# Decode attention of a hybrid decoder layer: one step list for three engines against a list for each, with the token transposes in another PSUM bank

## The reference

```
ckv_past = ckv_pool[page_table]; kpe_past = kpe_pool[page_table]
s = (q_abs . ckv_past + q_pe . kpe_past) * ATTN_SCALE
p = softmax(concat(s, s_new)); o_lat = p[past] . ckv_past + p[new] . ckv
```

```
sa = S . kk ;  S = S * d - sa x b + v x k ;  o = S . r
```

## Time and profile before

| | us |
|---|---|
| median of 3 runs (lowest, highest) | 2041.21 (2038.88, 2041.49) |
| profiled execution, its own time | 2037.07 |
| its span, first to last instruction | 2035.4 |
| TensorE busy | 1865.2 (92%) |
| VectorE busy | 895.6 (44%) |
| ScalarE busy | 494.7 (24%) |
| mean granted TensorE clock | 0.970 |

### The profile page before, as it was taken

The page is one execution under the profiler, slowest core; times in us unless marked ns, Lnnn a source line. Parts: engine busy times, 40 slices in busy tenths (PEclk is TensorE's granted clock), DMA queues, the critical chain, the costliest instruction groups (busy, mean ns, idle before and its releaser), DMA issues. The chain is left out here.

```text
span 2035.4 us, 45818 instructions
## 1 busy us (share of the span) xinstructions
PE 1865.2 (92%) x19360; PEld 1164.3 (57%) x19360; DVE 895.6 (44%) x1984; ACT 494.7 (24%) x1164; POOL 172.6 (8%) x158
## 2 busy tenths in 40 slices
PE   4899999999987999899949999999999879998898
PEld 2565676666654666654326656766666546665543
DVE  2024134222766676654230340332318577775542
ACT  3111012222412333311131110222224123333201
POOL 0010000011334000000000100000212240000000
PEclk9899999999999999979989999999999899999899
DMA  9500000000205666341075001010001166562411
GB/s 388 207 11 27 21 21 32 21 21 13 59 26 159 185 188 180 109 178 42 32 301 213 0 27 32 11 32 22 21 22 50 28 186 186 176 186 83 178 42 42
DMA packets 103927, 191.18 MB, mean 94 GB/s; under 512 B 17162, under 2 KB 87260, under 8 KB 100004
## 3 DMA queue, kind: packets, MB, share of 16 engines
q1 hardware_dynamic: 103716, 188.19, 27.9%
HBM read 175.41 MB, written 21.19 MB: 97 GB/s over the span
## 5 line engine op out<-in xcount | busy, mean ns | idle before, releaser
L771 PE MATMUL PB<-RB,R 128*128 128x344 f32 x1632 | 496.1, 457 | 0.0
L771 PEld LDWEIGHTS PB<-RB,R 128*128 128x128 f32 x1632 | 303.7, 191 | 159.6 <-issue 19.7
L1946 PE MATMUL PB<-RB,R 128*128 128x512 f32 x512 | 221.2, 593 | 0.0
L1589 PE MATMUL PB<-WUQ,Q 32*32 32x256 f32 x5120 | 191.0, 385 | 14.7 <-DVE WUQ L1748 9.4
L1748 DVE STREAM_TRANSPOSE WUQ<-RB 128x512 f32<-128x512 f32 x316 | 197.0, 676 | 5.5 <-DMA RB<-in_cache 5.3
L1946 PEld LDWEIGHTS PB<-RB,R 128*128 128x128 f32 x512 | 97.0, 190 | 120.8 <-issue 118.6
L931 ACT ACTIVATE R<-PB 128x344 f32<-128x344 f32 x90 | 41.2, 457 | 423.4 <-PE PB L771 423.4
L1184 DVE TENSOR_TENSOR PB<-PB,CST 128x128 f32<-128x128 f32 x64 | 18.8, 294 | 226.3 <-PE PB L791 226.3
L1589 PEld LDWEIGHTS PB<-WUQ,Q 32*32 32x32 f32 x5120 | 90.0, 104 | 46.0 <-DVE WUQ L1748 23.1
L619 PE MATMUL PB<-RB,R 128*128 128x344 f32 x288 | 88.5, 472 | 10.8 <-PEq L225 10.8
L619 PEld LDWEIGHTS PB<-RB,R 128*128 128x128 f32 x288 | 57.1, 199 | 41.4 <-issue 14.8
(11 more groups left out here) (355 smaller groups left out, 2619.6 us busy)
## 6 DMA issues: line engine op xcount, KB each, us to landing
RB<-in_cache SPq DMA_DIRECT2D x512, 160.0 KB, 2.6
R<-in_w_ada SPq DMA_DIRECT2D x16, 1536.0 KB, 17.4
R<-in_w_in SPq DMA_DIRECT2D x44, 512.0 KB, 3.7
RB<-in_w_out SPq DMA_DIRECT2D x8, 1024.0 KB, 9.9
RB<-out_x_stream SPq DMA_DIRECT2D x2, 4096.0 KB
out_x_stream<-RB SPq DMA_DIRECT2D x16, 512.0 KB
RB<-in_x_prompt SPq DMA_DIRECT2D x1, 4096.0 KB
RB<-in_w_kv SPq DMA_DIRECT2D x2, 1280.0 KB, 5.6
```

The source lines that it names most:

```text
L771: mm = pe.matmul(jobbank(j)[:, 0:CH], ring[:, blkno[n] % 4, k, :], hT[:, k, chunk(c)], start=(k == 0), stop=(k == KT - 1))
L1589: mm = pe.matmul(PB[qp[o], 2 * (h % 2) + q % 2, 0:256], Q4[qp[q], g, :], k[qp[q], c], start=(g == 0), stop=(g == NB - 1), skip_group_check ...
L1946: mm = pe.matmul(PB[0:n, 2 * (t % 2) + hf, :], mixT[:, k, cols(t)], wo[:, k, hf * 512:(hf + 1) * 512], start=(k == 0), stop=(k == 5))
```

## The change

The one list becomes three (`PE_PAIR`, `DVE_PAIR`, `ACT_PAIR`), each walked by its own engine, with the words of one pair of heads repeated 8 times; `PT-` and `PV-` are those of the odd head of the pair before, `PT0` and `PV0` those of the pair's even head, and `T20`, `T21` are the first two turns of the next pair. TA writes bank 4 and not bank 6. The scaling of the state into `Sg` becomes a step G of its own, without drains but in the last pair, and the second part of the level masks becomes a step LV. The page slots (`QS`, `HB`) and SyncE's list are as before.

```
-            STEPS = [...]
-            chain = ("Z", "U", "H", "O")
-            plan = []
...
+            chain = ("Z", "U", "H", "G", "O")
+            PE_PAIR = (
+                "S00 S01 S02 MA Z0 S03 S04 U0 PT- S05 S06 H0 X1 S07 Z1 Y1 S08 U1 S09 S10 H1 X2 PV- Y2 S11 S12 S13 OO "
+                "X3 S14 PT0 S15 Y3 S16 S17 X4 AK TA Y4 S18 TB S19 X5 PV0 Y5"
+            ).split()
+            DVE_PAIR = (
+                "T02 T03 T04 T05 T06 MA T07 LV H0 T08 T09 T10 Y1 G0 T11 T12 MX0 H1 T13 Y2 T14 T15 T16 T17 T18 Y3 T19 "
+                "T20 G1 AK Y4 T21 MX1"
+            ).split()
+            ACT_PAIR = (
+                "Z0 U0 MA PT- X1 Z1 U1 X2 EX0 OO X3 PT0 X4 TA TB X5 EX1 Y5"
+            ).split()
+            def pair_plan(words):
+                out = []
+                for p in range(NS):
+                    for w in words:
+                        if w[0] in "ST" and w[1] in "012":
+                            out.append((2 * p + int(w[1]), w[0], int(w[2])))
+                        elif w[:2] in ("PT", "PV", "MX", "EX"):
+                            out.append((2 * p - 1 if w[2] == "-" else 2 * p + int(w[2]), w[:2], 0))
+                        else:
+                            out.append((p, "rw", w))
+                return [x for x in out if 0 <= x[0] < NH] + TAIL
...
                         elif n == "TA":
-                            pe.wait_ge(ak_done, p + 1)
+                            pe.wait_ge(pp_done, 2 * p + 1)
                             for f in range(2):
-                                pe.transpose(PB[:, 6, f * P:(f + 1) * P], A2[...], ident)
+                                pe.transpose(PB[:, 4, f * P:(f + 1) * P], A2[...], ident)
...
                         elif n == "TB":
-                            pe.wait_ge(ta_done, p + 1)
+                            pe.wait_ge(ak_done, p + 1)
...
                         if n[0] == "Z":
+                            pe.wait_ge(ta_done, p + 1)
                             pe.wait_ge(tb_done, p + 1)
...
-                    for h, what, g in plan:
+                    for h, what, g in pair_plan(PE_PAIR):
...
                         (PT, TensorE)
                             if h:
                                 pe.wait_ge(pp_done, h)
+                            if h % 2:
+                                pe.wait_ge(ta_done, h // 2 + 1)
...
                         (VectorE)
                             dve.transpose(Tm..., Tc...).then_inc(tm_done, 1)
+                        elif n == "LV":
                             levels(2, LEVELS).then_inc(bm_done, 1)
...
+                        elif n[0] == "G":
+                            i = 2 * p + int(n[1])
                             if i + 1 < NCH:
-                                dve.drain()
+                                if p == NS - 1:
+                                    dve.drain()
                                 dve.tensor_tensor(Sg, S0[:, (i + 1) % 4], ecol..., ALU.mult)
+                                if p == NS - 1:
+                                    dve.drain()
...
-                        elif what == "S":
-                            if NB * h + g + 2 < NB * NH:
-                                turn(NB * h + g + 2)
+                        elif what == "T":
+                            turn(NB * h + g)
```

More of the change, by code:

```diff
@@ L1402, in bass_hybrid_trunk @@
             fcol = lambda rb: RP + 32 * rb if rb < 8 else 32 * (rb - 8)
-            STEPS = ["MA", "Z0", "X1", "U0", "Y1", "H0", "X2", "Z1", "Y2", "U1", "X3", "H1", "Y3", "OO",
-                     "X4", "AK", "Y4", "TA", "X5", "TB", "Y5"]
-            chain = ("Z", "U", "H", "O")
-            plan = []
[L1410 to L1421, removed]
@@ L1422, in bass_hybrid_trunk @@
-            plan += [(NH - 1, "PT", 0), (NS, "rw", "Z0"), (NH - 1, "PV", 0), (0, "FC", 1), (NS, "rw", "U0"), (0, "FC", 2), (NS, "rw", "H0"),
-                     (0, "FC", 3), (NS, "rw", "Z1"), (0, "FC", 4), (NS, "rw", "U1"), (0, "FC", 5), (NS, "rw", "H1"), (0, "FC", 6),
-                     (NS, "rw", "OO")]
+            chain = ("Z", "U", "H", "G", "O")
[3 more added lines that the diff above has]
+            ).split()
@@ L1426, in bass_hybrid_trunk @@
+            TAIL = [(NH - 1, "PT", 0), (NS, "rw", "Z0"), (NH - 1, "PV", 0), (0, "FC", 1), (NS, "rw", "U0"), (0, "FC", 2), (NS, "rw", "H0"),
+                    (NS, "rw", "G0"), (0, "FC", 3), (NS, "rw", "Z1"), (0, "FC", 4), (NS, "rw", "U1"), (0, "FC", 5), (NS, "rw", "H1"),
+                    (0, "FC", 6), (NS, "rw", "OO")]
             with nc.Block() as block:
@@ L1477, in prepare @@
                         elif n == "TA":
-                            pe.wait_ge(ak_done, p + 1)
+                            pe.wait_ge(pp_done, 2 * p + 1)
                             for f in range(2):
-                                pe.transpose(PB[:, 6, f * P:(f + 1) * P], A2[:, f, p * P:(p + 1) * P], ident)
+                                pe.transpose(PB[:, 4, f * P:(f + 1) * P], A2[:, f, p * P:(p + 1) * P], ident)
                             for f in range(2):
-                                mm = pe.transpose(PB[:, 6, (2 + f) * P:(3 + f) * P], pT[:, 2 + f, p * P + 1:(p + 1) * P + 1], ident)
+                                mm = pe.transpose(PB[:, 4, (2 + f) * P:(3 + f) * P], pT[:, 2 + f, p * P + 1:(p + 1) * P + 1], ident)
                             mm.then_inc(ta_full, 1)
                         elif n == "TB":
-                            pe.wait_ge(ta_done, p + 1)
+                            pe.wait_ge(ak_done, p + 1)
                             for f in range(2):
@@ L1645, in prepare @@
                             act.wait_ge(ta_full, p + 1)
-                            t6 = PB[:, 6, :].rearrange("p (v f w k) -> p v f w k", v=2, f=2, w=2)
+                            t4 = PB[:, 4, :].rearrange("p (v f w k) -> p v f w k", v=2, f=2, w=2)
                             for c in range(2):
                                 for w in range(2):
-                                    op = act.activation(TOK[k][hp[w], 0:2, 2 * c:2 * c + 2, :], t6[hp[c], :, :, w, :], ACT.Identity)
+                                    op = act.activation(TOK[k][hp[w], 0:2, 2 * c:2 * c + 2, :], t4[hp[c], :, :, w, :], ACT.Identity)
                             op.then_inc(ta_done, 1)
@@ L1677, in follow @@
                             act.activation(A3[:, :, p * P:(p + 1) * P], PB[:, 6, 0:2 * P].rearrange("p (f t) -> p f t", f=2), ACT.Identity).then_inc(oo_done, 1)
-                    for h, what, g in plan:
+                    for h, what, g in pair_plan(ACT_PAIR):
                         if what == "rw" and g[0] in chain:
@@ L1792, in follow @@
                             op.then_inc(st_done, 1)
+                        elif n[0] == "G":
+                            i = 2 * p + int(n[1])
                             if i + 1 < NCH:
-                                dve.drain()
+                                if p == NS - 1:
+                                    dve.drain()
                                 dve.tensor_tensor(Sg, S0[:, (i + 1) % 4], ecol[:, :, i + 1:i + 2].broadcast_to([P, 2, 64]), ALU.mult)
-                    for h, what, g in plan:
+                                if p == NS - 1:
+                                    dve.drain()
+                    for h, what, g in pair_plan(DVE_PAIR):
                         if what == "rw" and g[0] in chain:
```

## The result

| | before | after |
|---|---|---|
| median (lowest, highest), us | 2040.92 (2038.88, 2041.49) | 2165.31 (2159.60, 2167.62) |
| profiled execution, its span | 2037.07, 2035.4 | 2159.60, 2157.9 |
| mean granted TensorE clock | 0.970 | 0.936 |

The changed kernel takes 1.0611 times as long (95% interval 1.0593 to 1.0628). It was forecast at 2167, slower.

A forecast was written before the change was run, and what follows sets the result against it. Taken as bound by when pages come, through a ring of two loads in series: 2037.1 + 94.8 (ring) + 31 (lower clock) = 2163 us, with 4.1 for the median 2167; range 2108 to 2200.

The forecast's parts named there:

- Bound by when pages come: Decode stage: page loads start when PV frees their slot and take 15.9 us; slack before the turn is only 3.7 us.
- The ring: Decode stage: PV0, load, T10, PV-, load, T20, back to PV0; loads in series, 37.2 us a pair against 28.96.
- Its size: Length of a decode pair: two loads of 15.9 us, 5.4 from turns to PVs, 2.4 for the lower clock.
- The fixed point: First layer, counted from pair 0's T20 at 650.46: PV0 at 653.4, pair 7's T10 at 892.5; 47.4 us a layer.
- The clock: Decode steps after TensorE's stops run partly at the lower clock: 2.4 us a pair, 31 us in both layers.
- The 44 us that I worked out by its formula: Decode stages: clock loss of 26 stops by the skill's formula, 44 us in place of 31, so 2181.
- The smaller edits: Decode stage: three lists save up to 2.9 us a pair, single score blocks cost 0.4; all hidden while pages are late.
- "faster" rival: Decode stage: pages come in time, TensorE's waits decide, 46 us of waits go: 1995; chance 0.05.
- Short loads: Decode page loads: each takes the shortest seen, 14.3 us, and the clock stays up; 42 us less, 2094; chance 0.09.

## Why the prediction was right, step by step

- **Bound by when pages come.** Right. The slack before T10 and T20 (3.7 us in the pair read, 1.7 to 5.3 in all) was all there was; all 26 gated loads now end 0.12 to 0.13 us before the turn that waits for them, which is the hand-over alone.
- **The ring.** Right, and shown from four sides: open it at PV-, at PV0 or at T20 and 75 to 95 of the 125 us go; open it at both PVs and all go; shorten the loads and 26 times the shortening goes, and some of the clock's part with it. T10 was not moved by itself.
- **Its size.** 2 x 15.9 + 5.4 + 2.4 = 39.6 us a pair was forecast, 39.74 measured, but two parts missed and cancelled. The steps at the lower clock cost more: from PV to first issue 2.72 us in each load (1.94 before), and 6.95 us for the two ways from turn to PV (3.41 and 3.54), where 5.4 was priced at the upper clock. That is 3.1 us for the clock where 2.4 was taken. The loads took less: from first issue to last page 13.54 us (13.95 before), 0.8 us in a pair. That the total came within 2 us of 2167 is in part luck.
- **The fixed point.** T20 of pair 0 came at 648.89 (forecast 650.46), the first turn of the stage being 2.0 us sooner; PV0 followed at 652.3 (653.4), and T10 of pair 7 at 906.05 (892.5, and some 15.6 for the clock: 908).
- **The clock.** Right in kind. On the steps of the ring it cost 3.1 us a pair, some 40 us over 13 pairs, where 31 was taken; filling the stops gave 21 us net of longer loads. After every stop, not after 0.6 of them, 0.50 was granted: behind the 26 stops at gated turns for 3.4 us in 5 cases and for 6.8 in 21. The Trainium skill (TensorE: Matmul & The Clock Gate, "HAM oscillation — how this bites in real kernels") says that a DMA wait which comes back in each tile lets the clock fall again each time. The trace agrees, 26 times in 26. The 44 us that I worked out by its formula (2136 + 44 is 2180, not the 2181 written) took 3.4 us for every stretch; with the measured lengths, 160 us in all, the formula gives an estimate of 80 us, far above the 40 seen in the ring. Part of a low stretch passes while TensorE stands still (it is busy for 5.68 of the 6.80 us from 785.30), and part over steps behind PV's first half, which are not in the ring.
- **The smaller edits.** Wrong, where it did not count: I wrote that the three lists save up to 2.9 us of waits in a pair and that single blocks cost 0.4. With pages in time the waits are 0.9 us less and the stops marked "issue" 1.7 us more, and nothing that can be measured is saved (0.999). My "faster" rival at 1995 therefore never had its price, whatever the loads did.
- **Short loads.** The rival's 14.3 us didn't come; of the 1.6 us that it wanted a load was 0.4 us shorter from first issue to last page, and the lower clock before the first issue took that back twice over.

## What to carry to other kernels

When a step that frees a buffer is moved in a hand-written order, follow the buffer all the way round: free, load, first use, everything queued behind the first use, and back to the step that frees. If the sum of a round is longer than the period, the engines' busy shares say nothing; and where two buffers' rounds pass through each other's waiting instructions, their loads add. Put nothing that a later "free" depends on behind a first use in any queue: one turn moved past three steps gave 95 of 125 us. A free step also has an earliest place, behind the copy that it reads.

## What the runs showed of the hardware that was not expected

- The granted clock fell in a regular beat with the stops, in the stretches above 13.7 us at the upper and 6.8 at the lower level, and 18 products put into the stops of a pair kept it up and made the kernel faster by 21 us.
- The part of a load from first issue to last page took 13.5 us with TensorE standing still for much of it and 14.1 with the stops filled, the same DMAs in both. Of these 0.6 us, 0.4 lie between SyncE's first and last issue (10.3 and 10.7 us) and 0.2 behind the last issue. No run was made to find what makes them longer; it stays open.
- SyncE takes 0.33 us for the issue of most pages and 0.566 us from one to the next in the median, but now and then over 1 us for one, 2.0 at most: in 23 of the 384 issues of the 24 loads of the changed kernel, in 31 with the stops filled and 35 in the kernel before. What these are is open.
